# Three 512-token norms of a two-block transformer kernel, taken one stream at a time

## The reference

```python
def rms_norm(x, g):
    y = x * lax.rsqrt(jnp.mean(x * x, axis=-1, keepdims=True) + EPS)
    return y * g
# first block, each layer:
h = rms_norm(x, g_mix) * (1.0 + m_lat[1]) + m_lat[0]      # context likewise, with m_ctx
x = x + m_lat[2] * (mixers(h) @ w_out)
h = rms_norm(x, g_ffn) * (1.0 + m_lat[4]) + m_lat[3]
x = x + m_lat[5] * conv_ffn(h, ffn_up, ffn_conv, ffn_conv_b, ffn_down)
# second block: the same frame, gated delta rule in layer 0, gated linear attention (GLA)
# in layer 1, and a squared-ReLU network: square(relu(h @ w1)) @ w2
```

## Time and profile before

| | us |
|---|---|
| median of 3 runs | 2898.54 (2897.14 to 2901.67) |
| the profiled execution, its own time | 2900.53 |
| its span, first to last instruction | 2897.4 |
| TensorE busy | 2760.6, 95% of the span |
| VectorE / ScalarE / POOL busy | 1647.5 / 672.3 / 1078.1 |
| mean granted TensorE clock | 0.977 |

### The profile page before, as it was taken

How to read it: one execution, slowest core, us unless ns; L and a number is a source line. 1 busy time by engine, 2 the same in 40 slices (tenths; PEclk the granted TensorE clock), 3 DMA queues, 4 the chain that set the end, 5 groups by cost and what they waited for, 6 DMA issues and landing times.

```text
span 2897.4 us, 42849 instructions
## 1 busy us (share of the span) xinstructions
PE 2760.6 (95%) x16753; PEld 2293.7 (79%) x16753; DVE 1647.5 (57%) x2787; ACT 672.3 (23%) x1394; POOL 1078.1 (37%) x801
## 2 busy tenths in 40 slices
PE   6999999999899999999978999999999999999999
PEld 4765488888685899777558888886888886797898
DVE  3446478772355688588667776775454212333762
ACT  1124121110224221254345554311000002321100
POOL 3310154454320366334234442552555440020564
PEclk8999999999999999999989999999999999999999
DMA  7447222222426444543423332122222223111443
GB/s 298 186 183 271 102 88 88 88 87 91 157 86 264 176 159 169 193 182 151 150 55 84 89 70 84 73 87 73 88 88 87 88 88 121 59 44 59 146 170 122
DMA packets 108368, 357.92 MB, mean 124 GB/s; under 512 B 41201, under 2 KB 60401, under 8 KB 69137
## 3 DMA queue, kind: packets, MB, share of 16 engines
q1 hardware_dynamic: 86432, 334.65, 32.7%
q10 hardware_dynamic: 20160, 15.40, 1.6%
q0 software_dynamic: 1584, 5.21, 0.6%
HBM read 344.62 MB, written 10.62 MB: 123 GB/s over the span
## 4 chain that ended last, share of the span: by engine, by line
PE 82%; DVE 8%; ACT 4%; DVEq 2%; issue 2%; DMA 1%; ACTq 0%; POOLq 0%; SPq 0%; POOL 0%
PE psum L3175 42%; PE psum L234 9%; PE psum L1557 5%; PE psum L268 3%; PE psum L694 3%; PE psum L3168 3%; PE psum L2715 2%; DMA ring<-in_stream 1%; PE psum L1776 1%; PE psum L513 1%; PE psum L1758 1%; ACT h_sb L1178 1%; PE psum L2816 1%; PE psum L526 1%; PE psum L369 1%
## 5 line engine op out<-in xcount | busy, mean ns | idle before, releaser
L3175 PE MATMUL psum<-arena,ring 128*128 128x256 f32 (+1 forms) x3240 | 584.4, 333 | 0.9 <-DVE arena L3253 0.9
L3175 PEld LDWEIGHTS psum<-arena,ring 128*128 128x128 f32 x3240 | 510.1, 191 | 47.9 <-DVE arena L3253 1.5
L3175 PE MATMUL psum<-arena,c 128*128 128x256 f32 (+1 forms) x2032 | 377.6, 334 | 1.7 <-DVE c L3194 1.7
L3175 PEld LDWEIGHTS psum<-arena,c 128*128 128x128 f32 x2032 | 324.0, 191 | 33.7 <-issue 1.9
L3203 POOL TENSOR_TENSOR c<-ring 128x512 f32<-128x512 f32 (+1 forms) x79 | 102.8, 1301 | 548.8 <-PE psum L3175 296.1
L3205 POOL TENSOR_TENSOR ring<-ring 128x512 f32<-128x512 f32 (+1 forms) x167 | 255.0, 1527 | 30.9 <-issue 7.5
L3203 POOL TENSOR_TENSOR rows<-ring 128x512 f32<-128x512 f32 (+1 forms) x70 | 90.2, 1288 | 470.7 <-PE psum L3175 258.9
L3175 PE MATMUL psum<-h_sb,ring 128*128 128x256 f32 (+1 forms) x1376 | 252.9, 337 | 0.7 <-DVE arena L1125 0.7
L234 PE MATMUL psum<-h_sb,ring 128*128 128x256 f32 (+1 forms) x672 | 230.7, 502 | 19.6 <-ACT h_sb L1178 18.1
L3175 PEld LDWEIGHTS psum<-h_sb,ring 128*128 128x128 f32 x1376 | 220.6, 192 | 24.8 <-issue 3.5
L3219 ACT COPY kst<-psum 128x256 f32<-128x256 f32 (+1 forms) x112 | 36.5, 326 | 871.9 <-PE psum L3175 840.0
(11 more groups left out here) (396 smaller groups left out, 4937.2 us busy)
## 6 DMA issues: line engine op xcount, KB each, us to landing
ring<-in_stream SPq DMA_DIRECT2D x302, 1024.0 KB, 4.9
arena<-decays SPq DMA_DIRECT2D x24, 256.0 KB, 4.8
...
```

What stands on the lines that cost most here:

```text
L3175: ins = pe.matmul(dst, self.seven_weights(n, i, k, nk, w_sums), self.seven_moving(x, sums, i, k, nk, width), start=first and j == 0 and k ...
```

## The change

Norms 2, 5 and 6 are handled one stream at a time (`SPLIT_NORMS`); `SEVEN_NORMS` keeps norm 4. Since these norms now raise their semaphores once for each stream, `norms_before(k)` replaces the plain counts.

1. `pe_seven` gets an argument `norm`. With it, the last output tiles' chunks issue (1, 2), (7, 6), (4), (5, 3). After product 5 of the last group come the latent's two matmuls by ones (`pe_stream_sums`, 256 columns each), then product 3.
2. `dve_split_residual` takes the place of `dve_seven_residual` there: latent first through residual, square and norm, then the context.
3. The next stage's chunk 0 begins with the latent's columns. The context's sums stand inside it: before the fifth matmul of the latent's second half (norms 2 and 5) or before the second tile (norm 6). In the FFN behind norm 5 chunk 0 has 32 matmuls of 256 columns in place of 16 of 512.
4. `act_norm` runs Ln, Exp and the eight modulations once for each stream. At norm 2 its copy of the modulation rows stands between the two.
5. The four "gap2" chunks follow the last product directly. POOL's `load_nab` now waits for the context's sum.

```diff
-SEVEN_NORMS = (2, 4, 5, 6)
+SEVEN_NORMS = (4,)
+SPLIT_NORMS = (2, 5, 6)
+def norms_before(k):
+    return k + sum(split < k for split in SPLIT_NORMS)
+        def pe_stream_sums(pe, k, s):
+            part = slice(SEQ * s, SEQ * (s + 1))
+            n = norms_before(k) + s
+            if s == 1:
+                pe.wait_ge(S["n_rinv"], n)
+            pe.wait_ge(S["n_sq"], 2 * n + 1)
+            pe.matmul(bank(5)[:, part], ones[:, :], h[:, 0, part], start=True, stop=False)
+            pe.wait_ge(S["n_sq"], 2 * n + 2)
+            pe.matmul(bank(5)[:, part], ones[:, :], h[:, KT - 1, part], start=False, stop=True).then_inc(S["n_sum"], 1)
...
-        for pair, names in enumerate(((1, 2), (7, 6), (4, 5), (3,))):
+        for pair, names in enumerate(((1, 2), (7, 6), (4,), (5, 3)) if norm is not None else ((1, 2), (7, 6), (4, 5), (3,))):
...
+                if last and norm is not None and i == 5:
+                    b["pe_stream_sums"](pe, norm, 0)
...
-            pe_norm_sums(pe, 2, TOK)
+            for i in range(ada_count("gap2")):
+                pe_ada(pe, "gap2", i)
...
+                                    if 2 * li in SPLIT_NORMS and (c, half, tt, k) == (0, 0, 1, 4):
+                                        pe_stream_sums(pe, 2 * li, 1)
...
+            if rho == 1:
+                b["pe_stream_sums"](pe, 6, 1)
...
+            if norm in SPLIT_NORMS:
+                act_log_exp_set(act)
+                if mods is not None:
+                    act.wait_ge(S["mods_ready"], mods)
+                for s in range(2):
+                    if s == 1 and f"gap{norm}" in ADA_PARTS:
+                        act_ada_all(act, f"gap{norm}")
+                    part_s = slice(SEQ * s, SEQ * (s + 1))
+                    n = norms_before(norm) + s
+                    act.wait_ge(S["n_sum"], n + 1)
+                    act_rsqrt(act, rinv[:, part_s], bank(5)[:, part_s], 1.0 / D).then_inc(S["n_rinv"], 1)
+                    for kt in range(KT):
+                        hp = h[:, kt, part_s]
+                        act.wait_ge(S["n_normed"], KT * n + kt + 1)
+                        act.activation(hp, hp, ACT.Identity, scale=a_mul[:, l, part, kt, s:s + 1],
+                                       bias=mod[:, l, 3 * part * KT + kt, s:s + 1]).then_inc(S["h_ready"], 1)
+                return
...
+    def dve_split_residual(self, dve, n, item, l, norm, gate=5):
...
+        dve.tensor_tensor(u2, u1, product(1, 1), ALU.add)
+        dve.drain()
+        square(even, 0)
+        dve.tensor_tensor(u3, u2, product(1, 0), ALU.add)
+        dve.drain()
+        add_square(0)
+        dve.wait_ge(T["pairs_done"], 3 * item + 3)
+        dve.tensor_tensor(part(h, odd, 0), u3, product(2, 0), ALU.add)
+        dve.drain()
+        residual(odd, 0)
+        dve.drain()
+        square(odd, 0).then_inc(S["n_sq"], 1)
+        b["dve_stream_norm"](dve, norm, 0)
+        dve.wait_ge(S["products"], 2 * (n + 1))
...
```

More of the change, by code:

```diff
@@ L325, in pe_norm_sums @@
                     pe_ada(pe, gap, i)
-            added = 2 * k + 1
+            added = 2 * norms_before(k) + 1
             pe.wait_ge(S["n_sq"], added)
@@ L1014, in dve_ffn1_seven @@
             second.dve_sums(dve, act1[:, 16:22, :], act1_sums[2], 3)
-            for cp in range(OUT_CHUNKS):
+            for cp in range(OUT_CHUNKS - 1):
                 second.dve_seven_residual(dve, sched["1down0"][0] + FT_GROUPS * (cp + 1) - 1, FFA_ITEMS + UP_CHUNKS - 1 + cp, cp, 0)
+            second.dve_split_residual(dve, sched["1down0"][0] + FT_GROUPS * OUT_CHUNKS - 1, FFA_ITEMS + UP_CHUNKS + OUT_CHUNKS - 2, 0, 2)
         act1_half = area(0, FT * SEQ, k=FT)
@@ L1187, in dve_norm, with dve_stream_norm @@
                                   ALU.mult).then_inc(S["n_normed"], 1)
+        def dve_stream_norm(dve, norm, s):
+            part = slice(SEQ * s, SEQ * (s + 1))
+            dve.wait_ge(S["n_rinv"], norms_before(norm) + s + 1)
+            for kt in range(KT):
+                dve.tensor_tensor(h[:, kt, part], x[:, kt, part], rinv[:, part], ALU.mult).then_inc(S["n_normed"], 1)
         def dve_mods(dve, l, bias, m0, m1):
@@ L2468, in dve_delta @@
         n0 = b["sched"]["2out0"][0]
-        for cp in range(OUT_CHUNKS):
+        for cp in range(OUT_CHUNKS - 1):
             self.dve_seven_residual(dve, n0 + 2 * cp + 1, OUT0_ITEMS + cp, cp, 2, 2)
+        self.dve_split_residual(dve, n0 + 2 * OUT_CHUNKS - 1, OUT0_ITEMS + OUT_CHUNKS - 1, 2, 5, 2)
     def dve_between(self, dve, j, half):
@@ L3146, in seven_ready, with pe_seven @@
         return ready
-    def pe_seven(self, pe, n, chunk, item, x, sums, first=True, last=True, ready=None, nk=4, behind_first=None, width=SEQ, late=None, base=None, w_sums=None, token_major=False):
+    def pe_seven(self, pe, n, chunk, item, x, sums, first=True, last=True, ready=None, nk=4, behind_first=None, width=SEQ, late=None, base=None, w_sums=None, token_major=False, norm=None):
         b, T = self.b, self.S2
@@ L3313, in dve_seven_residual, with product, part, residual @@
                 residual(rho, KT - 2)
+    def dve_split_residual(self, dve, n, item, l, norm, gate=5):
+        b, S, T = self.b, self.b["S"], self.S2
+        h, x, mod = b["h"], b["x"], b["mod"]
+        u1, u2, u3, u4 = self.out1, self.out2, self.out3, self.out4
+        even, odd = KT - 2, KT - 1
+        def product(pair, j):
+            return self.seven_bank(item, pair)[:, SEQ * j:SEQ * (j + 1)]
+        def part(tile, rho, s):
+            return tile[:, rho, SEQ * s:SEQ * (s + 1)]
+        def residual(rho, s):
+            dve.scalar_tensor_tensor(part(x, rho, s), part(h, rho, s), mod[:, l, gate * KT + rho, s:s + 1], part(x, rho, s),
+                                     ALU.mult, ALU.add)
+        def square(rho, s):
+            return dve.tensor_tensor(part(h, rho, s), part(x, rho, s), part(x, rho, s), ALU.mult)
+        def add_square(s):
+            dve.tensor_tensor(part(h, 0, s), part(h, 0, s), part(h, even, s), ALU.add).then_inc(S["n_sq"], 1)
+        dve.wait_ge(T["first_copied"], item + 1)
+        dve.tensor_tensor(part(h, even, 0), u1, product(0, 1), ALU.add)
+        dve.drain()
+        residual(even, 0)
+        dve.wait_ge(T["pairs_done"], 3 * item + 2)
+        dve.tensor_tensor(u2, u1, product(1, 1), ALU.add)
[8 more added lines that the diff above has]
+        residual(odd, 0)
+        dve.drain()
+        square(odd, 0).then_inc(S["n_sq"], 1)
+        b["dve_stream_norm"](dve, norm, 0)
+        dve.wait_ge(S["products"], 2 * (n + 1))
+        dve.tensor_tensor(u4, u2, product(3, 0), ALU.add)
+        dve.tensor_tensor(part(h, odd, 1), u3, product(3, 0), ALU.add)
+        dve.drain()
+        dve.tensor_tensor(part(h, even, 1), u4, product(3, 1), ALU.add)
+        residual(odd, 1)
+        dve.drain().then_inc(T["products_read"], 1)
+        residual(even, 1)
+        square(odd, 1)
+        dve.drain()
+        square(even, 1)
+        dve.drain()
+        add_square(1)
+        dve.drain().then_inc(S["n_sq"], 1)
+        b["dve_stream_norm"](dve, norm, 1)
     def pe_out0(self, pe):
@@ L3351, in pe_ffn0 @@
         b["arrived"](pe, n0)
-        for half in range(2):
-            b["k_products"](pe, b["bank"](half), lambda k: b["w"][:, n0 % RING, k, half * 128:(half + 1) * 128],
-                            lambda k: h[:, k, :], ready=KT * 5 if half == 0 else None)
+        for s in range(2):
+            for half in range(2):
+                for k in range(KT):
+                    if half == 0:
+                        pe.wait_ge(S["h_ready"], KT * (norms_before(5) + s) + k + 1)
+                    if (s, half, k) == (0, 1, 4):
+                        b["pe_stream_sums"](pe, 5, 1)
+                    ins = pe.matmul(b["bank"](half)[:, SEQ * s:SEQ * (s + 1)], b["w"][:, n0 % RING, k, half * 128:(half + 1) * 128],
+                                    h[:, k, SEQ * s:SEQ * (s + 1)], start=k == 0, stop=k == KT - 1)
+                if s == 1:
+                    ins.then_inc(S["products"], 1)
         for c in range(1, UP2_CHUNKS):
```

68 lines of the change are left out of this document (35 added, 33 removed).

## The result

The changed kernel takes 2880.57 us (median of 4 runs, 2877.86 to 2884.09), beside 2899.26 for the kernel before: a ratio of 0.9935 (95% interval 0.9919 to 0.9951), 18.7 us less. The forecast was 2874.0 with a range of 2868 to 2885, so the sign and the range hold, and 5.8 of the 24.5 us of gain are missing. The profiled execution took 2884.09 (span 2882.2), the slowest of the four.

The account below looks back on a forecast made before the run. TensorE bounds the kernel, losing 36.9 us at three norm hand-overs. Gains of 9.3 (norm 2), 5.9 (norm 5) and 9.3 (norm 6) sum to 24.5 us, giving 2874.0 us, range 2868 to 2885.

Parts of the forecast that it names:

- Norm 6: Hand-over to the second GLA tile's end: 25.6 us becomes 16.3, gain 9.3; the rest of the context hidden by later tiles.
- Norm 5: Hand-over to the end of the feed-forward part's chunk 0: 31.1 us becomes 25.2, gain 5.9.
- E: Zero point of the hand-over times: the end of product 7, at norms 5 and 6 of product 6.
- POOL hits none: At norm 5's context, POOL's sums delay no norm pass, chunk 0 ends at 23.3 us; with three hit, 26.0.
- Norm 2: Hand-over to the projection's chunk 0 end: 37.9 us becomes 28.6, gain 9.3, with 3.8 us waiting for weights.
- norm 4's row: Profile row behind norm 4: TensorE waited for weights and its clock stayed 1.00; cited as evidence against the clock rival.
- the clock rival: A low-clock stretch of 7 us remains in each hand-over, costing 3.5 us each: 2884.5 us; chance 12%.
- The rival's case for norm 2 alone: DMA waits lower TensorE's clock at norm 2 only, losing some 3.5 us: 2877.5 us.
- the 36.9 us: Time lost before the change over three hand-overs: 14.8 at norm 2, 10.3 at norm 5, 11.8 at norm 6.
- Gives its gain back: Norm 2's 9.3 us is lost again as the attention stage waits for later `load_nab` and POOL work: 2883.3; 7%.
- Doesn't start earlier: Context sums inside the first chunk stall TensorE, so pauses only change place: 2898.5 us; chance 3%.
- VectorE at POOL's pace: 26 VectorE operations per hand-over slow to 1.49 us from 0.42, adding 28 us; 2902 through norm 5; chance 3%.

Follow-up runs that it names:

- after: Profiled execution of the changed kernel's first group of runs, no further edit: 2884.09 us, the slowest of four; that group's median is 2880.57 us.
- all_again: The changed kernel run again with no edit, for a second trace: median 2880.93 us, ratio 0.9945 to the kernel before; profiled execution 2871.78 us.
- third: The changed kernel run once more with no edit, for a third trace: 2877.43 us, ratio 0.9930 to the kernel before.
- pool_late: Changed kernel, but at norm 5 POOL starts its four sums of weights only after the last norm pass: 2877.77 us, ratio 0.9929 to the kernel before.
- fill_fit: Changed kernel plus 9 and 5 unread constant matmuls in norm 2's two waits for weights: 2874.13 us, ratio 0.9923 to the kernel before.
- fill: Changed kernel plus unread constant matmuls: 16 and 9 at norm 2's waits, 8 and 18 at the second attention stage's start: 2879.44 us, ratio 0.9927.
- rho2: Changed kernel, but at norm 6 the context's sums stand behind the whole second GLA tile: 2883.95 us, ratio 0.9942 to the kernel before.
- only_norm5: Only norm 5 split by streams, norms 2 and 6 as in the kernel before: 2891.94 us, ratio 0.9981 to that kernel.

## Why the prediction was right, and where it was wrong

- **Norm 6 (9.3): right, 9.3 measured**, with the sums behind product 5, the first GLA matmul 0.5 us behind product 3 (0.8 foreseen) and the wait of 1.16. The claim that the rest is well hidden was wrong in its size: 0.3 us of cover, not 4.7, so that nothing was lost behind was luck.
- **Norm 5 (5.9): right, 6.3 measured** in after (24.8 from E, as in all_again and third). The choice between "POOL hits none" (23.3) and "three" (26.0) was 25.2; it is 24.8 with two passes' worth of stretching (4.96 us for eight against 2.77, so 2 x 1.07), and without POOL 22.9. pool_late is a direct test. Without POOL it is 0.4 shorter than the forecast's 23.3, since the context's first matmul starts 15.5 after E and not 16.0. The rule cited from the Trainium skill ("SBUF — State Buffer"), that the two lock each other out for a whole instruction, fits both numbers: the longest pass 1.48, against an estimate of at most 1.7 by the rule, and the median, 0.41, not stretched at all.
- **Norm 2 (9.3): the step that failed.** The chain and the loads were right: waits of 2.29 and 1.00 us (2.2 and 1.6 foreseen), chunk 0 at 12.9 (12.7). Wrong was the clock, "granted clock 1.00 throughout". The gain was 6.75, 6.0 and 5.9 in three executions of the changed kernel. The forecast held norm 4's row against the clock rival: TensorE waited for weights and stayed at 1.00. That row was one execution, and a weak witness. Norm 4 too has two waits with one narrow chunk between, but mostly shorter ones: up to 0.6 us, then 1.4 to 1.6. Twelve of the 14 traces kept their clock behind them (the 32 records took 14.3 to 14.7 us). In after (second wait 2.33 us; 0.79 from 1192 to 1200) and all_again (0.62 and 1.42 us; 0.79 from 1187 to 1195) it fell, and they took 15.7. At norm 2 the waits are 2.2 to 2.6 and 0.7 to 2.6 us, and there the clock fell in each of the six executions whose waits weren't filled. fill_fit gives the price: 2.3 us beside after; by the first 24 records of chunk 0 (7.31 to 8.47 us in the six, 5.45 in fill_fit) it is 1.9 to 3.0, where the rival said 3.5. The rival's case for norm 2 alone (2877.5) has the step that the traces show. The Trainium skill ("TensorE: Matmul & The Clock Gate", HAM oscillation) warns of low clocks behind DMA waits; the traces agree at norm 2, six of six, and at norm 4 in two of 14. At norms 5 and 6 of after, all_again and third, where the pauses are 0.5 to 1.2 us, it stayed at 1.00. It isn't safe there: behind ScalarE's gaps at norm 5's context it fell in fill (0.64 from 2014 to 2018), rho2 (0.59 from 2018 to 2022) and only_norm5 (0.68 from 2022 to 2026), whose hand-overs took 26.2, 26.2 and 26.6 us. That is three of the eight executions with norm 5 by streams and POOL's early start, and none of the three in which POOL starts later.
- **The rest of the missing 5.8.** By the hand-overs the change is worth 22.3 us in after, and measured by the runs 16.5 to 22.1. Of the remainder, after's trace shows 4.7 us at the attention stage and 2.0 at norm 4, stages whose code is as it was; low clocks make up 5.9 of these 6.7, and norm 4's longer wait 0.8. The profiled execution of after gained 5.9 less than its hand-overs, and that of all_again 7.2 more (2900.53 - 2871.78 = 28.8, hand-overs 21.5). A forecast of the steps doesn't hold that part. That the median came within the range needed its width: 2878.6 over all 15 runs, 4.6 above the forecast. The hand-overs kept 14.6 of the 36.9 us in after, where 12.5 were forecast and more than 18 would have proved it wrong.
- **The other rivals.** "Gives its gain back" fell with all_again. `load_nab` started at 759.05 and its 9.82 us lay beside chunks 0 and 1; TensorE's timeline shows no wait from 761 to 799. "Doesn't start earlier" and "VectorE at POOL's pace" fell with the timelines: two passes were stretched at norm 5 (the eight took 4.96 us), and none at norm 6 (2.77).
